# First norm's sums on TensorE, late loads issued by SyncE, and the second weight block rounded between the two halves of the input, in a four-layer model kernel

## The reference

```
mod = silu(c) @ ada_w + ada_b                      # one row, 3072 numbers
shift, scale, gate = split(mod, 3)
h = x * rsqrt(mean(x*x, channels) + EPS) * norm_g * (1 + scale) + shift
proj = h @ w_in                                    # 1024 x 2464
...                                                # latent, neighbourhood and differential attention
x = x + gate * (y @ w_out)
```

## Time and profile before

| | us |
|---|---|
| three runs, median | 4526.33 |
| lowest and highest | 4509.15, 4529.17 |
| the profiled execution, its time | 4515.78 |
| its span in the trace | 4513.6 |
| PE busy | 4214.3 (93%) |
| VectorE, ScalarE, POOL busy | 2035.8, 1576.6, 480.2 |

### The profile page before, as it was taken

How to read it: one execution, slowest core, us unless ns; L and a number is a source line. 1 busy time by engine, 2 the same in 40 slices (tenths; PEclk the granted TensorE clock), 3 DMA queues, 4 the chain that set the end, 5 groups by cost and what they waited for, 6 DMA issues and landing times.

```text
span 4513.6 us, 54083 instructions
## 1 busy us (share of the span) xinstructions
PE 4214.3 (93%) x22424; PEld 3240.3 (72%) x22424; DVE 2035.8 (45%) x3109; ACT 1576.6 (35%) x2468; POOL 480.2 (11%) x477
## 2 busy tenths in 40 slices
PE   4998899898998899999999869999999999999999
PEld 2777666576776676677763456888888888888887
DVE  2235776533234685544235573333334553333344
ACT  3325665423324565432336423311213332212132
POOL 2010000102001000101005651000000320000010
PEclk8999999999998899999999979999999999999999
DMA  3120000043111000003110000111111101111112
GB/s 143 53 70 21 21 1 1 11 184 105 47 56 41 21 1 1 1 29 121 49 38 1 40 1 28 56 47 47 48 55 47 66 19 54 50 47 47 47 47 84
DMA packets 46915, 208.37 MB, mean 46 GB/s; under 512 B 14672, under 2 KB 15312, under 8 KB 25552
## 3 DMA queue, kind: packets, MB, share of 16 engines
q1 hardware_dynamic: 18576, 135.27, 8.5%
q10 hardware_dynamic: 28096, 69.64, 4.4%
HBM read 188.12 MB, written 12.58 MB: 44 GB/s over the span
## 4 chain that ended last, share of the span: by engine, by line
PE 87%; DVE 5%; ACT 3%; issue 2%; ACTq 1%; POOL 1%; DMA 0%; DVEq 0%; POOLq 0%
PE ps L674 13%; PE ps L1229 12%; PE ps L1230 12%; PE ps L1228 12%; PE ps L1056 3%; PE ps L907 3%; PE ps L909 2%; PE ps L908 2%; PE ps L1045 2%; PE ps L766 2%; PE ps L782 2%; PE ps L978 2%; PE ps L963 2%; PE ps L797 1%; PE ps L1065 1%
## 5 line engine op out<-in xcount | busy, mean ns | idle before, releaser
L1228 PE MATMUL ps<-n_hi,w_hi 128*128 128x512 f32 x1280 | 500.7, 391 | 0.0
L1230 PE MATMUL ps<-n_hi,w_lo 128*128 128x512 f32 x1280 | 498.7, 390 | 0.0
L1229 PE MATMUL ps<-n_lo,w_hi 128*128 128x512 f32 x1280 | 498.6, 390 | 0.0
L1228 PE MATMUL ps<-m_hi,w_hi 128*128 128x512 f32 x1152 | 450.4, 391 | 0.0
L1230 PE MATMUL ps<-m_hi,w_lo 128*128 128x512 f32 x1152 | 448.8, 390 | 0.0
L1229 PE MATMUL ps<-m_lo,w_hi 128*128 128x512 f32 x1152 | 448.7, 390 | 0.0
L1374 ACT ACTIVATE w_hi<-w 128x2048 fp32r<-128x2048 f32 x103 | 196.9, 1912 | 446.7 <-DMA w<-in_wstream 446.5
L2028 DVE TENSOR_TENSOR w_lo<-w,w_hi 128x2048 fp32r<-128x2048 f32 x103 | 237.0, 2301 | 152.5 <-ACT w_hi L1374 152.4
L2772 DVE TENSOR_TENSOR m<-ps,arena 128x512 f32<-128x512 f32 x128 | 88.5, 692 | 433.4 <-ACT arena L1938 433.4
L1938 ACT ACTIVATE arena<-ps 128x512 f32<-128x512 f32 x128 | 76.5, 598 | 585.1 <-PE ps L1230 585.1
L1228 PEld LDWEIGHTS ps<-n_hi,w_hi 128*128 128x128 f32 x1280 | 240.4, 188 | 50.8 <-issue 1.2
(11 more groups left out here) (382 smaller groups left out, 8273.4 us busy)
## 6 DMA issues: line engine op xcount, KB each, us to landing
w<-in_wstream SPq DMA_DIRECT2D x121, 1024.0 KB, 4.8
arena<-in_wstream ACTq DMA_DIRECT2D x17, 1024.0 KB, 4.8
out<-h ACTq DMA_DIRECT2D x48, 256.0 KB, 2.0
h<-in_na_bias ACTq DMA_DIRECT2D x6, 1152.0 KB, 7.5
m<-in_wstream SPq DMA_DIRECT2D x4, 1024.0 KB, 8.9
h<-in_xT ACTq DMA_DIRECT2D x2, 2048.0 KB, 34.8
arena<-in_wstream SPq DMA_DIRECT2D x4, 1024.0 KB, 19.4
h<-in_xT ACTq DMA_DIRECT2D x4, 1024.0 KB, 10.9
```

The lines of the kernel that those rows point to most:

```text
L1228: mm(dst, wb[0][:, k, wcols], hi[:, k, :], start=(g == 0), stop=False)
L1229: mm(dst, wb[0][:, k, wcols], lo[:, k, :], start=False, stop=False)
L1230: last = mm(dst, wb[1][:, k, wcols], hi[:, k, :], start=False, stop=(g == KT - 1))
```

## The change

- **Start, loads.** g2 is issued before x; rope_cos and rope_sin move to SP, behind the second streamed block; the first streamed block is issued before the last two ada blocks. ScalarE's first exp follows the issue of x directly.
- **Start, norm.** POOL adds nothing. PE sums each squared half tile as it comes, eight matmuls accumulated for each half (bank 4, bank 5), with four buffers (`first_sq`); half 0 stands between ada blocks 3 and 4, half 1 between 5 and 6. The two roots and the rounding of block 0 come on ScalarE before `ada_row` 6 and 7. The sum for lambda comes first.
- **Half 1 in the two layers.** VectorE makes it as it makes half 0 (`normed_tile`), each followed by the low part of the tile before; ScalarE rounds it with the shift in one instruction. POOL has no part in it.
- **Second block.** ScalarE rounds block 1 after its eight roundings of half 0, VectorE takes the rest after the low parts of half 0. In the even stage ScalarE rounds it before the root of half 1, VectorE takes its rest before half 1, and `normed_tile` and `rest` of half 1 alternate.
- **Differential attention.** ScalarE only raises `na_over`; SP, behind the load of the twelfth streamed block of the layer (`DIFFERENTIAL_AT`), waits for it and issues the four copies and eight loads.

```diff
-        self.converts = {0: 1, 6: 2}
+        self.converts = {6: 2}
...
+        def first_sq(i):
+            return (lay_ring if i % 4 < 2 else lay_stat)[:, i % 2, :]
...
+            def differential_loads(layer):
+                sp.wait_ge(sems["na_over"], layer + 1)
+                for x, y in zip(df_sw[1], (df_qk[:, 1, :], df_qk[:, 3, :])):
...
             for b in range(ADA_FIRST):
+                if b == ADA_FIRST - 2:
+                    streamed(0)
                 sp.dma_start(ada_first[b], a["wstream"][b].rearrange("p (k n) -> p k n", k=KT))\
                   .then_inc(sems[f"ada_first{b // 2}"], 16)
...
+            streamed(1)
+            sp.dma_start(rope_cos[:, :], a["rope_cos"]).then_inc(sems["rope_in"], 16)
+            sp.dma_start(rope_sin[:, :], a["rope_sin"]).then_inc(sems["rope_in"], 16)
+            for j in range(2, len(STREAMED)):
+                streamed(j)
+                if j in DIFFERENTIAL_AT:
+                    differential_loads(DIFFERENTIAL_AT[j])
...
+            lam_sums(0)
             for b in range(ADA_FIRST + 1):
+                if b in (4, 6):
+                    hf = b // 2 - 2
+                    for k in range(KT):
+                        i = KT * hf + k
+                        pe.wait_ge(sems["lay_sq"], i + 1)
+                        mm(ps[:, 4 + hf, :], ones, first_sq(i), start=(k == 0), stop=(k == KT - 1)).then_inc(sems["first_sum"], 1)
...
-            lam_sums(0)
-            for hf in range(H2):
-                root_sums(0, hf)
...
+            def first_square(i):
+                k, hf = FIRST_ROOTED[i]
+                if k == 0:
+                    act.wait_ge(sems[f"h_in{hf}"], 16)
+                if i >= 4:
+                    act.wait_ge(sems["first_sum"], i - 3)
+                nc.scalar.activation(first_sq(i), half(h, k, hf), ACT.Square).then_inc(sems["lay_sq"], 1)
+
             for b in range(ADA_FIRST):
+                if b in (4, 6):
+                    for k in range(KT):
+                        first_square(KT * (b // 2 - 2) + k)
+                if b == 6:
+                    round_block()
+                    norm_root(0, 0)
+                    norm_root(0, 1)
                 ada_row(b, b % 4)
...
+                    for hf in range(H2):
+                        if hf and layer:
+                            norm_root(layer, 1)
+                        for k in range(KT):
+                            act.wait_ge(sems["n0_done"], KT * (2 * layer + hf) + k + 1)
+                            nc.scalar.activation(half(n_hi_m, k, hf), half(n, k, hf), ACT.Identity, bias=shift[:, k:k + 1])\
+                                .then_inc(sems["x_hi"], 1)
+                        if hf == 0:
+                            round_block()
...
-                for x, y in zip(df_sw[1], (df_qk[:, 1, :], df_qk[:, 3, :])):
...
+                act.sem_inc(sems["na_over"], 1)
...
             with T.span(**EVEN_COUNTS.totals):
+                round_block(w_hi_m)
                 norm_root(L, 1)
...
+                    for k in range(KT):
+                        input_low(k, 0)
+                    block_rest()
+                    if layer == 0:
+                        dve.wait_ge(sems["rope_in"], 32)
+                    for k in range(KT + 1):
+                        if k < KT:
+                            normed_tile(layer, k, 1)
+                        if k:
+                            input_low(k - 1, 1)
...
-            root_additions(0)
             for layer in range(L):
-                with T.span(v1_done=KT):
-                    pool.wait_ge(sems["lay_rstd"], 2 * layer + 2)
-                    for k in range(KT):
-                        G.tensor_tensor(out=n[:, k, HALF:S], in0=h[:, k, HALF:S], in1=lay_stat[:, 1, :], op=ALU.mult)\
-                            .then_inc(sems["v1_done"], 1)
```

More of the change, by code:

```diff
@@ L331 @@
 OUT_ORDER = [(x.tile, x.hf) for x in END if x.kind == "out"]
-ROOTED = [[(k, hf) for hf in range(H2) for k in range(KT)], OUT_ORDER, OUT_ORDER]
+ROOTED = [[], OUT_ORDER, OUT_ORDER]
+FIRST_ROOTED = [(k, hf) for hf in range(H2) for k in range(KT)]
 ROOT_ADDITION, ROOT_ADDED = _additions(ROOTED)
@@ L364 @@
 BANDED = 160
+LAYER_STREAMED = LAYER1_BLOCKS - ADA_BLOCKS
+DIFFERENTIAL_AT = {LAYER_STREAMED * layer + LAYER_STREAMED - GATE_BLOCKS - OUT_BLOCKS + 1: layer for layer in range(L)}
 def _na_unit(j, t):
@@ L1388, in norm_root @@
             def norm_root(u, hf):
-                act.wait_ge(sems["lay_ss"], 2 * u + hf + 1)
+                if u:
+                    act.wait_ge(sems["lay_ss"], 2 * (u - 1) + hf + 1)
+                else:
+                    act.wait_ge(sems["first_sum"], 2 * KT)
                 root(ps[:, 4 + hf, :], lay_stat[:, hf, :], lay_stat[:, hf, :], 1.0 / D, "lay_rstd")
@@ L1601, in _ @@
[L1601 to L1608, removed]
-            for layer in range(L):
-                with T.span(**LAYER_COUNTS.totals, v1_done=KT):
-                    for k in range(KT):
[L1612 to L1623, removed]
@@ new lines, in _ @@
+            for layer in range(L):
+                with T.span(**LAYER_COUNTS.totals):
+                    for hf in range(H2):
[7 more added lines that the diff above has]
+                            round_block()
@@ L1686, in _ @@
                 T["restored"].up(KT)
-                for x, y in zip(df_sw[1], (df_qk[:, 1, :], df_qk[:, 3, :])):
[L1688 to L1693, removed]
-                for j in range(2):
-                    act.dma_start(lt_wq[:, :, 64 * j:64 * j + 64], up[:, :, j, 0:MLA_NOPE]).then_inc(sems["lat_w"], 16)
-                    for i in range(2):
-                        act.dma_start(lt_wq[:, :, P + 64 * j + 32 * i:P + 64 * j + 32 * i + 32], up[:, :, j, MLA_NOPE:MLA_QK])\
-                            .then_inc(sems["lat_w"], 16)
+                act.sem_inc(sems["na_over"], 1)
                 U = DF_U
@@ L2299, in _, with input_low @@
                 normed_tile(0, k, 0)
[L2300 removed]
             for layer in range(L):
[L2302 to L2303 removed]
+                with T.span(**LAYER_COUNTS.totals, x_split=2 * KT):
+                    def input_low(k, hf):
                         dve.wait_ge(sems["x_hi"], T.next("x_hi"))
[L2305 to L2306 removed]
+                        V.scalar_tensor_tensor(out=half(n_lo, k, hf), in0=half(n, k, hf), scalar=shift[:, k:k + 1],
+                                               in1=half(n_hi_m, k, hf).bitcast(F32), op0=ALU.add, op1=ALU.subtract)\
                             .then_inc(sems["x_split"], 1)
                     for k in range(KT):
[L2309 removed]
+                        input_low(k, 0)
+                    block_rest()
+                    if layer == 0:
[5 more added lines that the diff above has]
+                            input_low(k - 1, 1)
                     C = LAYER_COUNTS
@@ L2452, in _ @@
                     rest(half(n_lo, k, 0), half(n, k, 0), half(n_hi_h, k, 0)).then_inc(sems["x_split"], 1)
-                for k in range(KT):
-                    normed_tile(L, k, 1)
-                for k in range(KT):
-                    rest(half(n_lo, k, 1), half(n, k, 1), half(n_hi_h, k, 1)).then_inc(sems["x_split"], 1)
+                block_rest(w_hi_m)
+                for k in range(KT + 1):
+                    if k < KT:
+                        normed_tile(L, k, 1)
+                    if k:
+                        rest(half(n_lo, k - 1, 1), half(n, k - 1, 1), half(n_hi_h, k - 1, 1)).then_inc(sems["x_split"], 1)
                 C = EVEN_COUNTS
```

39 lines of the change are left out of this document (21 added, 18 removed).

## The result

| | before | after |
|---|---|---|
| median of the runs beside each other, us | 4523.82 (4509.15 to 4529.17, 4 runs) | 4474.66 (4467.08 to 4482.58, 4 runs) |
| profiled execution, us | 4515.78 | 4479.18 |
| its span, us | 4513.6 | 4477.3 |

The changed kernel takes 0.9897 of the time before, 95% interval 0.9866 to 0.9928: faster by 1.0%, with 4494.4 us forecast and 4474.66 measured. From profile to profile the gain is 36.6 us (31.9 forecast), from median to median 49.2.

A forecast was written before the change was run, and what follows sets the result against it. PE, holding 87% of the span, was taken as the bound, with its waits at five places to shorten. 12.2 + 4.8 - 0.2 + 15.1 = 31.9 us off the median 4526.3 gave 4494.4 us, range 4480 to 4514.

The forecast's parts named there:

- The start: Start up to the first projection's third group: first matmul at 65.4, group 2 at 85.5; gain 12.2 us.
- Layer 1: Layer 1's projection: PE's pause before group 2 shortens from 10.3 to some 5.5 us; gain 4.8 us.
- The even stage: Even stage's projection: early rest of block 1 buys nothing, group 0's square takes its place; -0.2 us.
- The differential attention: Differential attention's start in both layers: first exp earlier by 7.6 and 7.4 us, together 15.1 us.
- An ada block with its row: Start: each ada block with its row takes 1.53 us, the price used for ada rows 4 to 7.
- the median 4526.3: Whole kernel: median of the earlier runs, from which the 31.9 us gain was taken to get 4494.4 us.
- Rival 1: Start: PE stays at its lower clock through the 16 sums; 15.1 us less gain, 4509.5 us; chance 0.12.
- rival 2: Start: issuing x's second half holds ScalarE to about 31 us; gain 25, 4501 us; chance 0.10.
- Rival 3: Differential attention: its start does not move, because a DMA, PE or SP holds it; 4509.5 us; chance 0.06.
- Rival 4: Three starts: VectorE becomes the bound, 61 small instructions at 1.7 us cost 64 us; 4558 us; chance 0.03.
- The range's low end: Whole kernel: the fastest time the prediction's range allowed, 4480 us.

The follow-up runs named there:

- the two profiles with idle matmuls: Kernel before plus idle TensorE matmuls in the first four units of each differential stage, profiled twice; 4508.27 us median of 12 runs, ratio 0.9989.
- The 25 idle matmuls: Kernel before with idle matmuls in its differential stages, plus 25 float32 matmuls while PE waits ahead of the ada products; 4496.83 us, ratio 0.9965.
- the later execution of before: Kernel before, unchanged, profiled a second time: 4533.11 us.

## Why the prediction was wrong in size, step by step

**The start: right for the execution it was made from.** First exp at 10.25 (8 to 12 forecast). Half 0 of x landed at 36.3, not 34.5. The eight sums took 9.51 and 7.13 us (9.0 and 6.9 worked out). First projection matmul at 67.7 against 65.4, third group at 86.30 against 85.5. With the slower first group behind it, the next group came at 94.22 after 105.67 before (99.35, a group of 5.47 and a sum of 0.86): 11.4 us gained, 12.2 forecast. Of the 2.3 us by which the first matmul was late, a pause of 4 us instead of 6 made up most.

**Layer 1: 6.2 us gained, 4.8 forecast.** From the projection's first matmul to group 2 it is 27.5 us before and 22.2 after, 5.3 less, and the first group behind the shorter pause took 6.11 instead of 7.02, 0.9 less.

**The even stage: 1.8 us gained, a loss of 0.2 forecast.** Group 2 came 22.79 us after the first matmul against 22.89, as worked out. But its first group took 6.91 us where it had taken 8.57; the prediction gave no price to that restart.

**The differential attention: the start moved as forecast.** The first exp comes 2.43 us after the scores' start instead of 10.08, 7.65 us against 7.6; in layer 1 it is 2.43 instead of 9.81, 7.4 as forecast. The Trainium skill's rule ("DMA: Bandwidth & Descriptors", "Issuing engines are not separate DMA queues"), that moving the issues saves only the issuing time, usually small beside the transfer, would have left the whole at 16.8 us; the runs with only the loads moved gained 20 [11, 29] by themselves. It was issuing time that was saved, as the rule says, but it was not small: twelve issues in a row held ScalarE for 10 us while its first exp was due.

**The step that failed** is the start's "An ada block with its row comes every 46.96 - 45.42 = 1.53 us", taken as a property of the kernel before, and with it the sum made "from the median 4526.3". Two things were wrong there.

1. Of the kernel before's start there are two outcomes, and the profiled one was the quick one. In the other six of the eight blocks come every 2.81 us, and the first projection ends 8.7 us later (331.3 against 322.6; 7.9 between the two profiles with idle matmuls). It showed in three of the six profiles with this start. The new start takes both courses, too, and neither costs it anything: its blocks 2 and 3 took 1.93 us in six of the nine profiles with the new start and 1.07 in three, but x's load was the longer way in all nine, and the first sum began between 36.8 and 37.3 us. Its blocks 4 to 7 come right behind eight sums and took 1.07 in all nine. With the layers' part, too (eight of them), the first projection matmul stands between 66.5 and 68.3. So the start's term, 12.2 in the prediction, is 11.4 against one execution of before and 20.1 against the other. The 25 idle matmuls support it by trial: with them the median fell by 11.4 us and the mean by 10.5 (4507.0 to 4496.5). The start explains a part of that. If the seven slower of those twelve runs were the ones with the slow start, which no profile of them shows, it gave 7/12 x 7.9 = 4.6 on average, and the earlier end of the quick outcome 1.1. The other 5 are not explained.

2. The median of three runs was 10.6 us above the mean of 70. The profiled execution, 4515.78, happened to lie at that mean. From it, 31.9 less would have been 4483.9, inside the range, and 9.7 above the changed kernel's mean of 4474.2.

So of the 19.7 us between forecast and result 10.6 are the starting point and 9.6 are size (41.5 less 31.9), less 0.4 by which the result's median lies above the mean. The steps as the profiles show them sum to 11.4 + 6.2 + 1.8 + 15.0 = 34.4 us, close to the 33.6 between the kernels with a quick start on both sides; that is 2.5 of the 9.6, from layer 1 and the even stage. The other 7.1 are not measured one by one. The second outcome of the start would be some 4 of them if it comes in half of the runs of before, as in three of six profiles.

One more place can hold the rest. From the end of the first projection to the first differential scores it took 162.3, 162.3 and 159.2 us in the three profiles with the slow start, 153.1 to 158.4 in the four with the quick one, and 150.5 to 155.4 in the nine with the changed start. In a window over the neighbourhood attention of layer 0 the granted clock was 0.90 in the later execution of before and 0.96 in the first (148.0 and 138.6 us, 970 and 971 matmuls). So an execution with the slow start loses up to 9 us there as well, and the changed kernel has not shown that. Why the one goes with the other was not tried.

The 36.2 us between the spans of the two profiles are not simply the 34.4 of the steps with something added: the ways from the differential scores to the next projection gave -1.6 and 13.6 us, together 12.0 and not 15.0, and the ways ahead of these scores -0.2 and 4.4.

**The rivals.** Rival 1 (lower clock through all sums) did not come: 0.86 us a sum after the first ones. In rival 2 the second half of x did not hold ScalarE past 10.2. Rival 3 fell with the exp at 466.82. Rival 4 fell with eight normed tiles in 5.39 us and pairs at 1.33 us. The range's low end failed because it had a bound for every new cost and none for how differently the kernel before can run.

## What to carry to other kernels

A gain read from one profile is a gain against that execution. Where PE was idle ahead of a chain that sets the end, look in a second profile whether the same matmuls have the same durations, and give the range the difference. Ask, too, which of the old kernel's costs the new one hides: work moved under a load that it waits for anyway loses its slow outcome as well as its duration. And a new wait named in a prediction (the square behind eight roundings) is the next edit: it gave some 15 us for one reordered instruction in each projection.

## What the runs showed of the hardware

- The same instructions of the same program took 10.1 us in one execution and 15.2 in another, from 34 us on, with PE idle before. After 24 us of idle matmuls they took 8.4 (4.3 + 4.1) in the one execution profiled, and all twelve runs lay within 12.7 us.
- The granted clock read 1.00 from 34 to 48 us in both. In the slow one it still read 1.00 at 60 to 85 us with PE mostly idle, and at 93.3 us with matmuls of 0.63 to 0.80 us, where the quick one read 0.50 for the like.
- What a us at half clock costs depends on the stage. By estimate it is 0.3 us in the differential stage, where VectorE is busy for 133 of 151 us (161.7 against 150.9 us). An execution with a stretch of 27.3 us at half clock, PE busy throughout, took 10.4 us longer from the even projection on than one without it, of a kernel that differs in five loads.
- The same issue can be short or long by what stands before it: in the kernel before the two issues of x took 5.68 us together, and the next large one after them, rope_cos, 22.86; on SP, with no load of x ahead of it in that engine's own line, the issue of rope_cos took 1.41. Four swaps in layer 0 took 2.86 us on SP and 2.95 on ScalarE, so SP was no quicker at it; it only had nothing else to do.
